# The prompt recurrence of a hybrid decoder step: key groups of 32 on four column groups, decays on the queries, output gate on VectorE

## What is computed

```python
cum = cumsum(log(f))                             # along the tokens of a chunk
decay = exp(where(t >= s, cum[t] - cum[s], NEG)) # per key dimension
att[t,s] = sum_k q[t,k] * k[s,k] * decay[t,s,k]
o = att @ v + (q * exp(cum)) @ S
S = exp(cum[last]) * S + (k * exp(cum[last] - cum)).T @ v
o = rmsnorm(o, gnorm) * silu(hg)                 # hg: the output gate
```

## Time and profile before

| | |
|---|---|
| median of 3 runs | 2823.49 us (2822.08 to 2826.85) |
| the profiled execution | 2820.2 us, its span 2818.4 us |
| stage of the change | 1545 to 1749 us of the span |
| TensorE busy | 2326.8 us (83%) |
| VectorE busy | 1400.5 us (50%) |
| ScalarE busy | 995.1 us (35%) |
| GpSimd busy | 235.8 us (8%) |
| mean granted clock of TensorE | 0.885 |

### The profile page before, as it was taken

One profiled execution on the slowest core, in us unless ns is written; L12 is line 12 of the kernel. 1 busy time (PEld: TensorE's weight loads), 2 busy tenths in 40 slices (PEclk: granted clock), 3 DMA queues, 4 the chain that ended last, 5 costly groups with the idle time before them and its releaser, 6 DMA issues.

```text
span 2818.4 us, 34190 instructions
## 1 busy us (share of the span) xinstructions
PE 2326.8 (83%) x12790; PEld 1822.4 (65%) x12790; DVE 1400.5 (50%) x2176; ACT 995.1 (35%) x1265; POOL 235.8 (8%) x193
## 2 busy tenths in 40 slices
PE   8999999958988878888886088898962999999980
PEld 8999999954434365656654087554531888888870
DVE  4311233124555434444443765242342999999974
ACT  3111111112222323332332512211421877777762
POOL 0000000001121100000000200100002111111102
PEclk9999999958998979999897567799975999999995
DMA  4232333350000053333332301542215999999957
GB/s 158 112 127 75 111 120 128 111 158 27 8 5 8 12 217 128 127 128 128 128 128 81 112 12 58 150 163 83 89 62 201 412 412 415 414 414 411 413 235 283
DMA packets 109189, 462.59 MB, mean 164 GB/s; under 512 B 21088, under 2 KB 53904, under 8 KB 91208
## 3 DMA queue, kind: packets, MB, share of 16 engines
q1 hardware_dynamic: 73544, 321.77, 29.9%
q0 software_dynamic: 12448, 93.35, 8.1%
q10 hardware_dynamic: 23104, 46.20, 4.4%
HBM read 389.11 MB, written 79.05 MB: 166 GB/s over the span
## 4 chain that ended last, share of the span: by engine, by line
PE 69%; DVE 11%; DMA 9%; issue 5%; ACT 3%; POOL 1%; SPq 1%; ACTq 1%; DVEq 0%; POOLq 0%; PEldq 0%
PE ps L252 11%; PE ps L254 11%; PE ps L253 11%; PE ps L2398 4%; PE ps L1457 4%; PE ps L2323 4%; PE ps L1958 3%; DMA arena<-in_cache_slc,arena 3%; PE ps L1105 2%; PE ps L1087 2%; DVE c_x_low L1668 1%; DMA arena<-in_rope 1%; PE ps L2816 1%; PE ps L1493 1%; PE ps L1583 1%
## 5 line engine op out<-in xcount | busy, mean ns | idle before, releaser
L2948 DVE TENSOR_TENSOR e_low<-e_raw,e_high 128x2048 fp32r<-128x2048 f32 x192 | 430.5, 2283 | 55.7 <-ACT e_high L2886 55.7
L2886 ACT ACTIVATE e_high<-e_raw 128x2048 fp32r<-128x2048 f32 x192 | 356.7, 1912 | 18.9 <-ACT arena L2905 18.9
L252 PE MATMUL ps<-e_high,e_x_high 128*128 128x512 f32 x512 | 203.2, 397 | 10.1 <-DVE e_low L2948 7.5
L254 PE MATMUL ps<-e_high,e_x_low 128*128 128x512 f32 x512 | 200.9, 392 | 0.0
L253 PE MATMUL ps<-e_low,e_x_high 128*128 128x512 f32 x512 | 200.5, 392 | 0.0
L252 PE MATMUL ps<-h_high,wc_high 128*128 128x352 f32 x576 | 187.8, 326 | 1.3 <-ACTq L610 1.3
L253 PE MATMUL ps<-h_low,wc_high 128*128 128x352 f32 x576 | 186.2, 323 | 0.0
L254 PE MATMUL ps<-h_high,wc_low 128*128 128x352 f32 x576 | 185.9, 323 | 0.0
L252 PE MATMUL ps<-w_high,h_high 128*128 128x256 f32 (+1 forms) x576 | 174.0, 302 | 7.8 <-DVE w_low L436 4.9
L254 PE MATMUL ps<-w_high,h_low 128*128 128x256 f32 (+1 forms) x576 | 173.0, 300 | 0.0
L253 PE MATMUL ps<-w_low,h_high 128*128 128x256 f32 (+1 forms) x576 | 172.9, 300 | 0.0
(11 more groups left out here) (530 smaller groups left out, 4759.6 us busy)
## 6 DMA issues: line engine op xcount, KB each, us to landing
e_raw<-in_w_gate SPq DMA_DIRECT2D x32, 2048.0 KB, 10.0
e_raw<-in_w_up SPq DMA_DIRECT2D x32, 2048.0 KB, 9.5
e_raw<-in_w_down SPq DMA_DIRECT2D x32, 2048.0 KB, 10.5
scratch_yb<-arena ACTq DMA_DIRECT2D x32, 512.0 KB, 11.2
scratch_zT<-arena ACTq DMA_DIRECT2D x24, 528.0 KB, 2.7
wc_raw<-in_w_cols SPq DMA_DIRECT2D x24, 512.0 KB, 5.4
arena<-in_x_all SPq DMA_DIRECT2D x18, 512.0 KB, 3.5
scratch_yb<-arena SPq DMA_DIRECT2D x16, 512.0 KB, 5.5
```

Of the source, the lines that this page charges most:

```text
L252: nc.tensor.matmul(out, ah, bh, start=start, stop=False)
L254: return nc.tensor.matmul(out, al, bh, start=False, stop=stop)
L2886: nc.scalar.activation(high[m][:, c], raw[m][u][:, c], ACT.Copy).then_inc(high_ready[m], 1)
L2948: nc.vector.tensor_tensor(low[m][u][:, c], raw[m][u][:, c], high[m][:, c].bitcast(F32), ALU.subtract).then_inc(split_ready[m], 1)
```

## The change

The keys of a tile are taken in four groups of 32 (`G = 4`, `GS = 32`), and the products of a group write 32 partitions of the result: weights of 32 columns instead of 128, group by group on a column group of its own. Between groups, the queries are decayed instead of the keys: `qR`, 3 copies of the 128 queries of a head, 384 elements; within a group, two products of 16 queries each use a prepared buffer `near` (3 halves of 16 keys per group). A head has 3 products for later groups (96, 64 and 32 queries) and 8 of 16 queries, a tile 44 products. VectorE clears two banks of the result once. GpSimd has no work in the stage any more: VectorE multiplies the gate tile by tile; the gain goes to the next stage, where ScalarE applies it as a scale while it evicts the turned rows, after a small transpose and copy of the gain. ScalarE takes the gate's sigmoid after the logarithms, VectorE scales the queries after the scans. TensorE's loop over tiles is written out. In the next stage the load of `gn` is first in ScalarE's queue.

```diff
-    ek, ecum, key, q, qh, v, gate, kd = (k.buf(HH, SEQ) for _ in range(8))
-    kh_flat = k.buf(2 * HH * NS * P + P)
+    G, GS = 4, 2 * SUB
+    ek, ecum, key, q, qh, v, gate, sg = (k.buf(HH, SEQ) for _ in range(8))
+    near = k.buf(HH, 3 * SEQ // 2)
+    qR = k.buf(2, HH, (G - 1) * P)
-    R = k.buf(HH, QT, NS + 1, NS)
+    R, Rl = k.buf(HH, QT, (G - 1) * NS), k.buf(HH, QT, G)
...
-    def gpsimd(pool):
-        pool.wait_ge(consts, 48)
-        pool.wait_ge(gate_sigmoid, 1)
-        nc.gpsimd.tensor_tensor(flat(gate), flat(gate), flat(kd), ALU.mult).then_inc(gated, 1)
-        pool.wait_ge(gated, 1)
-        g = flat(gate).rearrange("p (t n) -> p t n", n=P)
-        nc.gpsimd.tensor_tensor(g, g, bc(gn, 1, HH * QT), ALU.mult).then_inc(gated, 1)
...
-        nc.scalar.activation(flat(qh), flat(q), ACT.Sigmoid).then_inc(q_sigmoid, 1)
-        act.wait_ge(gate_loaded, 16)
-        nc.scalar.activation(flat(kd), flat(gate), ACT.Sigmoid).then_inc(gate_sigmoid, 1)
+        nc.scalar.activation(flat(sg_q), flat(q), ACT.Sigmoid).then_inc(q_sigmoid, 1)
         for h in range(HH):
             act.wait_ge(key_ready, h + 1)
             nc.scalar.activation(ek[:, h], ek[:, h], ACT.Ln, ...).then_inc(log_ready, 1)
-        act.wait_ge(gated, 1)
+        act.wait_ge(gate_loaded, 16)
+        nc.scalar.activation(flat(sg), flat(gate), ACT.Sigmoid).then_inc(gate_sigmoid, 1)
         for h in range(HH):
             act.wait_ge(diffs_ready, h + 1)
-            nc.scalar.activation(kd[:, h], qh[:, h], ACT.Exp, scale=-1.0).then_inc(kd_ready, 1)
+            for a in range(2):
+                ins = nc.scalar.activation(z[:, :, 2 * a], own[:, :, a], ACT.Exp, scale=-1.0)
+            ins.then_inc(near_ready, 1)
+            nc.scalar.activation(z[:, :, 1], z[:, :, 1], ACT.Exp)
...
         def inside(i, u):
             for h in range(HH):
-                pe.wait_ge(kh_ready, HH * i + h + 1)
-                for n in range(NS):
-                    ins = nc.tensor.matmul(ps[:, u, h * P + SUB * n:h * P + SUB * (n + 1)], kh[:, u, h, n],
-                                           qh[:, h, bass.ds(i * P + SUB * n, SUB)], start=True, stop=True)
+                pe.wait_ge(qR_ready, HH * i + h + 1)
+                for g in range(G - 1):
+                    nc.tensor.matmul(ps[g * GS:(g + 1) * GS, u, h * P + (g + 1) * GS:(h + 1) * P],
+                                     ek[:, h, bass.ds(i * P + g * GS, GS)],
+                                     qR[:, u, h, g * P + (g + 1) * GS:(g + 1) * P], start=True, stop=True)
+                for a in range(2):
+                    for g in range(G):
+                        at = g * GS + a * SUB
+                        ins = nc.tensor.matmul(ps[g * GS:(g + 1) * GS, u, h * P + at:h * P + at + SUB],
+                                               near[:, h, bass.ds((i * G + g) * 3 * SUB + a * SUB, GS)],
+                                               qh[:, h, bass.ds(i * P + at, SUB)], start=True, stop=True)
...
-        each_tile(pe, outputs)
+        for i in range(QT):
+            outputs(pe, i, i % 2, i // 2, i < QT - 1)
...
-        dve.wait_ge(consts, 48)
+        nc.vector.memset(ps[:, 0:2], 0.0)
...
-        dve.wait_ge(q_sigmoid, 1)
-        step(nc.vector.scalar_tensor_tensor(out=flat(q), in0=flat(qh), scalar=DK ** -0.5, in1=flat(q), ...))
+        dve.wait_ge(consts, 32)
...
+        dve.wait_ge(q_sigmoid, 1)
+        step(nc.vector.scalar_tensor_tensor(out=flat(q), in0=flat(sg_q), scalar=DK ** -0.5, in1=flat(q), ...))
         for h in range(HH):
             dve.wait_ge(exps_ready, h + 1)
             nc.vector.tensor_tensor(ek[:, h], ek[:, h], key[:, h], ALU.mult)
-            nc.vector.tensor_tensor(kd[:, h], kd[:, h], key[:, h], ALU.mult)
+            for a in range(3):
+                nc.vector.tensor_tensor(z[:, :, a], z[:, :, a], k2[:, :, a // 2], ALU.mult)
             ins = nc.vector.tensor_tensor(qh[:, h], qh[:, h], q[:, h], ALU.mult)
-        for n in range(NS):
-            ins = nc.vector.memset(R.rearrange("p h t a b -> p (h t) a b")[:, :, n, n:NS], 0.0)
...
-                tile_steps(nc.vector.tensor_tensor(kh[:, u, h].rearrange("p n (j s) -> p n j s", s=SUB), ...))
-                nc.vector.tensor_copy(own, kd[:, h, tile(i)].rearrange("p (j s) -> p j s", s=SUB)
-                                      ).then_inc(kh_ready, 1)
+                nc.vector.tensor_tensor(qR[:, u, h].rearrange("p (g n s) -> p g n s", g=G - 1, s=SUB),
+                                        bc(t, 1, G - 1), ..., ALU.mult).then_inc(qR_ready, 1)
...
             if more:
-                factors(i + 1, 1 - u, Steps(dve, tile_step, HH, i + 1))
+                factors(i + 1, 1 - u)
+            g = by_tile(gate)[:, bass.ds(i, 1), :].rearrange("p o n -> p (o n)")
+            nc.vector.tensor_tensor(g, g, by_tile(sg)[:, bass.ds(i, 1), :].rearrange("p o n -> p (o n)"), ALU.mult
+                                    ).then_inc(gated, 1)
...
 def merge_stage(k, d, ident, route):
...
     def scalar(act):
+        act.dma_start(gn, d["gnorm"].partition_broadcast(N).rearrange("p o n -> p (o n)")).then_inc(gain_loaded, 16)
...
+        act.wait_ge(gain_ready, 1)
         for t in range(QT):
             act.wait_ge(transposed, t + 1)
             nc.scalar.activation(oT[:, 1, :, t * P:(t + 1) * P], ps[:, t % 4].rearrange("p (c n) -> p c n", c=4),
-                                 ACT.Copy).then_inc(rows_turned, 1)
+                                 ACT.Copy, scale=gcol[:, 0:1]).then_inc(rows_turned, 1)
...
     def tensor(pe):
+        pe.wait_ge(gain_loaded, 16)
+        nc.tensor.transpose(ps[:, 7, 0:N], gn, ident[0:N, 0:N]).then_inc(gain_turned, 1)
...
     def vector(dve):
         nc.vector.memset(mT[:, :, NTOK:TPAD], 0.0)
+        dve.wait_ge(gain_turned, 1)
+        nc.vector.tensor_copy(gcol, ps[:, 7, 0:N]).then_inc(gain_ready, 1)
...
-            step(nc.vector.tensor_tensor(sg, sg, bc(gn, 1, HH), ALU.mult))
```

More of the change, by code:

```diff
@@ L1879, in sync @@
         sp.dma_start(q, d["zT"][0:HH, :, 0:SEQ].rearrange("h p n -> p h n")).then_inc(q_loaded, 16)
-        for to, src in ((reset, d["reset"]), (tri, d["tri"]),
-                        (gn, d["gnorm"].partition_broadcast(P).rearrange("p o n -> p (o n)"))):
+        for to, src in ((reset, d["reset"]), (tri, d["tri"])):
             sp.dma_start(to, src).then_inc(consts, 16)
@@ new lines, in vector @@
+            nc.vector.tensor_tensor(near[:, h].rearrange("p (g a s) -> p g a s", a=3, s=SUB)[:, :, 1],
+                                    c2[:, :, 1, SUB // 2 - 1:SUB // 2].broadcast_to([P, NG4, SUB]), c2[:, :, 0],
+                                    ALU.subtract)
+            ends = ecum[:, h].rearrange("p (t g s) -> p t g s", g=G, s=GS)[:, :, :, GS - 1:GS].rearrange(
+                "p t g o -> p t (g o)")
+            middles = ecum[:, h].rearrange("p (t n s) -> p t n s", n=NS, s=SUB)[:, :, :, SUB // 2 - 1:SUB // 2].rearrange(
+                "p t n o -> p t (n o)")
@@ L2022, in vector @@
             nc.vector.tensor_scalar(r, r, 0.0, None, ALU.min).then_inc(diffs_ready, 1)
+        dve.wait_ge(q_sigmoid, 1)
+        step(nc.vector.scalar_tensor_tensor(out=flat(q), in0=flat(sg_q), scalar=DK ** -0.5, in1=flat(q),
+                                            op0=ALU.mult, op1=ALU.mult))
         for h in range(HH):
             dve.wait_ge(exps_ready, h + 1)
+            z = near[:, h].rearrange("p (g a s) -> p g a s", a=3, s=SUB)
+            k2 = key[:, h].rearrange("p (g a s) -> p g a s", a=2, s=SUB)
@@ L2041, in factors @@
-                own = kh_flat[:, at:at + NS * (P + SUB)].rearrange("p (n x) -> p n x", n=NS)[:, :, 0:SUB]
-                nc.vector.tensor_copy(own, kd[:, h, tile(i)].rearrange("p (j s) -> p j s", s=SUB)
-                                      ).then_inc(kh_ready, 1)
+                t = qh[:, h, tile(i)].rearrange("p (n s) -> p n s", s=SUB)
+                r = R[:, h, bass.ds(i, 1)].rearrange("p o (g n) -> p (o g) n", g=G - 1)
+                nc.vector.tensor_tensor(qR[:, u, h].rearrange("p (g n s) -> p g n s", g=G - 1, s=SUB), bc(t, 1, G - 1),
+                                        r.unsqueeze(3).broadcast_to([P, G - 1, NS, SUB]), ALU.mult
+                                        ).then_inc(qR_ready, 1)
@@ L2068, in one_tile @@
             dve.wait_ge(stored[u], 16 * r + 16)
-            g = by_tile(gate)[:, bass.ds(i, 1), :].rearrange("p o n -> p (o n)")
+            dve.wait_ge(gated, i + 1)
             for h in range(HH):
@@ L2074, in one_tile @@
             ins.then_inc(o_ready, 1)
-        dve.wait_ge(gated, 2)
-        factors(0, 0, Steps(dve, tile_step, HH, 0))
+        dve.wait_ge(gate_sigmoid, 1)
+        factors(0, 0)
         each_tile(dve, one_tile)
     recip_ready = sem("recip_ready")
-    k.stage(sync=sync, tensor=tensor, scalar=scalar, vector=vector, gpsimd=gpsimd)
+    k.stage(sync=sync, tensor=tensor, scalar=scalar, vector=vector)
 def merge_stage(k, d, ident, route):
@@ L2272, in scalar @@
```

(9 more changed lines are left out.)

65 lines of the change are left out of this document (30 added, 35 removed).

## The result

The changed kernel takes 2741.12 us, the median of 4 runs (2740.06 to 2743.73), beside 2825.17 for the kernel before in the same series: a ratio of 0.9698, 95% interval [0.9674, 0.9723]. The profiled execution took 2743.73 us, its span 2741.5, TensorE's mean granted clock 0.894.

The account below looks back on a forecast made before the run. VectorE was taken to bound the part before the tiles, TensorE the first inside and seven tiles. Terms -17.4, -8.9 and -40.9 sum to -67.2 us on 2820.2, 2753.0; with 3.3 for the median 2756, range 2746 to 2782.

Parts of the forecast that it names:

- Before the tiles: Stretch before the first tile, where TensorE does nothing: six terms on VectorE's path, together -17.4 us.
- the scans' 14.8: Before the tiles: without GpSimd's products the first two scans fall from 17.09 to 2.33 us, -14.8 us.
- the query product's 4.4: Before the tiles: the query product, formerly within a wait for the logarithms, now stands after the scans, +4.4 us.
- a sign of being wrong: Next stage's start: TensorE waiting for its gain would show the forecast wrong; the gain's wait was expected to be covered.
- The products of a tile: TensorE's narrow products: 88 records at L1583's price, 4.95 us cold, 2.5 to 3.7 warm; first inside -8.9 us.
- The seven tiles: Tiles after the first inside: bound passes to VectorE, first tile 9.5 us, six at 8.0, together 57.5, -40.9 us.
- The last tile: Last tile, 7.72 us: hangs on outputs, root and VectorE, which stay, so no change.
- The clock at 0.50 throughout (1): Seven tiles: clock stays at 0.50, 78.4 us, -20.0 instead of -40.9; whole time 2777, or 2782; chance 0.16.
- No overlap across column groups (2): TensorE's narrow products: a record costs as before, 0.139 warm and 0.216 cold; +11 us, 2835; chance 0.03.
- A weight load that waits for the product before it (3): TensorE's narrow products: loads wait even for other columns, 2.2 us per head cold; whole time 2765; chance 0.07.
- Another cause for the long scans (4): Before the tiles: scans are long for another reason than GpSimd, +14.8 on the sum, 2771 us; chance 0.02.
- Drains at changes of tiling: TensorE switching between 128-column and 32-column products: up to 0.35 us per change, 16 changes, 5.6 us; taken as nothing.

Follow-up runs that it names:

- the first experiment: The kernel before, with GpSimd's two products of 4,096 elements done by VectorE instead; ratio 1.0001 [0.9976, 1.0026] to the kernel before.

## Why the prediction was right and wrong

**Right** were the mechanism and its order: what bounds each part, GpSimd as the cause of the long scans, the pass of the bound to VectorE, and the clock's rise. Before the tiles -17.4 was forecast and -18.0 came: the scans' 14.8 and the query product's 4.4 are in the rows, the scans' start moved by 7.4, and from the first scan on ScalarE never held VectorE. The 0.6 beyond it is mostly the differences: 6.05 us per head instead of 6.24, where nil was put. The gain cost the next stage nothing, though TensorE did wait for it, which the prediction had named as a sign of being wrong: it idled 8.55 us for the gain where it had idled 9.88 for its rows before, and the stretch up to its first wide products took 28.35 us, 28.2 before. (The gain's load stands ahead of ten others, eight of which it had stood behind, not of six.)

**Wrong** was the step "The products of a tile": "I take L1583, which is nearest in shape", 0.056 us per record cold, 4.95 for the first inside, "warm I set 2.5 (half) to 3.7". The records cost 0.024 and 0.013, and TensorE is busy for 2.28 us of the first inside; its 2.66 to the mask are VectorE's, a bound that this step had put on TensorE alone. The working had the means to see it: the earlier trace rows 0.056 is a quarter of a 128-column record's 0.223, so L1583 shows the pace of 128 moving columns on four groups, not that of the weights. The busiest group of the change streams 256 columns per head, 0.43 to 0.45 us and 1.7 to 1.8 for four heads. That is 2.3 us in the first inside.

The larger part, 7.5 us, is in "The seven tiles". VectorE's tile was put at 7.8 and six tiles at 8.0; they average 7.03, and 6.84 is a tile at full clock without table loads. "Four products of 384, 0.56 each, spaced as now: 2.4" took over a spacing that held a wait between product and copy; without the copy they follow at 0.47 and take 1.87. The gate's product cost 0.60, not 0.7, neighbours overlapping. The rest came to 4.37 instead of 4.68, and the 0.2 of waiting wasn't there. The first tile, put midway between cold and warm at 9.5, took 7.72. The last tile, "nil", lost 1.2: it ran at 1.00, at 0.79 before.

So the stage is 11.6 us under its sum. The 3.1 us before it and the 5.0 after it, neither forecast, leave 9.7 of the span, and 9.3 on the profiled execution, which has 0.4 us more around its span than before. The prediction added 3.3 us for the step from the profiled execution to the median, as in the kernel before; the median of the changed kernel lies 2.6 below its profiled one. These 5.9 us are scatter between executions and no effect of the change: 15 in all. The range's lower end had the same fault as the centre: its "all tiles at 7.75" and "a first inside at 3.7" were still above what came.

**The rivals.** The clock at 0.50 throughout (1) fell: 0.95 over the seven tiles, though the first two had 0.87 and 0.78. No overlap across column groups (2) fell: 0.013 to 0.024 a record, where it needed 0.133. A weight load that waits for the product before it (3) wanted 2.2 us a head cold; 0.53 came, and even on a single group it was 1.49. The Trainium skill ("TensorE: Matmul & The Clock Gate", Part 3, The mechanism) lets loads overlap only where row groups differ; here all products use all rows, and the measured price contradicts it: 0.53 us for a head's 22 loads and 640 columns. Another cause for the long scans (4) fell with the first experiment. Drains at changes of tiling were put at nothing, with up to 0.35 us a change as the upper bound. No run isolated them, but the trace bounds them: in the warm tile shown above the first narrow record starts 0.205 us after the last wide one, where wide ones start 0.112 apart, and the first wide one 0.114 after the last narrow one. That is some 0.1 us a change, in a tile in which TensorE has 2 us to spare. A kernel with TensorE's loop still rolled was not tried.

## What to carry to other kernels

Before taking a price from a similar line, ask what sets that line's pace: divide its record by the streaming time of its columns, and if that explains it, the line says nothing about a shape with fewer. Count the columns of the busiest column group, not the average over the groups. Price instructions that follow one another by their distance from start to start, and take out the waits that the change removes. Where TensorE isn't the bound but its clock decides, judge an edit by the clock of every tile as well: a gain elsewhere can be eaten by the clock, and a slower order of products can make the stage shorter.

## What was unexpected

- A record with 32 columns of weights and 16 to 96 moving columns costs 0.013 us at full clock when four column groups take turns, against 0.139 for one of 128 columns of weights.
- A VectorE product that meets a GpSimd product doesn't slow down in part: it took 9.79 us instead of 1.22, and ended 1.1 us after GpSimd's.
- Removing 5.8 us before the tiles won nothing in the profiled execution, where three tiles then ran at 0.60 instead of one (16.72 us each instead of 13.62).
- Making TensorE's part of a warm tile longer, 5.51 us instead of 4.80, made the stage shorter: 118.8 instead of 120.2 (one profile each; the whole times don't separate the two).
- ScalarE's hardware loop loaded its two tables in every pass, 3 times 2 x 1.28 us. Written out it loaded one, once, and VectorE's wait for the root was gone from the later tiles.
